# Query and key projections of a pair of heads: seven block products in place of eight

## What is computed

```
hp = rms_norm(xp, norm_mix[0]);  hs = rms_norm(xs, norm_mix[0])
qkv = (xn @ w_qkv).reshape(b, t, 3, N_HEADS, HEAD_DIM)
s = einsum('bqhd,bkhd->bhqk', q, k) * HEAD_DIM ** -0.5 + bias
p = softmax(where(valid, s, neg));  out = einsum('bhqk,bkhd->bqhd', p, v)
x = x + out @ w_o
```

## Time and profile before

| | us |
|---|---|
| median of 3 runs | 1238.0 (1237.76 to 1239.86) |
| profiled execution, its own time | 1235.93 |
| its span in the profile | 1234.1 |
| TensorE busy, over the span | 1059.1 (86%) |
| VectorE busy | 497.5 (40%) |
| ScalarE busy | 295.3 (24%) |
| GpSimd busy | 281.1 (23%) |
| mean granted TensorE clock | 0.944 of 2.4 GHz |

### The profile page before, as it was taken

The page is one execution under the profiler, slowest core; times in us unless marked ns, Lnnn a source line. Parts: engine busy times, 40 slices in busy tenths (PEclk is TensorE's granted clock), DMA queues, the critical chain, the costliest instruction groups (busy, mean ns, idle before and its releaser), DMA issues.

```text
span 1234.1 us, 14547 instructions
## 1 busy us (share of the span) xinstructions
PE 1059.1 (86%) x5320; PEld 619.8 (50%) x5320; DVE 497.5 (40%) x1063; ACT 295.3 (24%) x647; POOL 281.1 (23%) x286
## 2 busy tenths in 40 slices
PE   6999999999997898878874998998996889888880
PEld 5777777776454433333323776764545333333330
DVE  3144434335346311111117598996457111011117
ACT  3223223233211111111002555555111111111002
POOL 3100000000000420110143298990002211110143
PEclk9999999999997998999996998999997999998995
DMA  8973222411716799999995284100018999999994
GB/s 274 383 229 113 78 75 77 131 58 58 314 67 243 276 419 420 420 417 420 420 383 159 75 322 139 50 1 25 35 39 314 406 419 421 390 421 421 420 386 159
DMA packets 109501, 304.79 MB, mean 247 GB/s; under 512 B 17314, under 2 KB 64546, under 8 KB 85737
## 3 DMA queue, kind: packets, MB, share of 16 engines
q1 hardware_dynamic: 87769, 253.95, 53.5%
q0 software_dynamic: 21520, 49.88, 11.1%
q10 hardware_dynamic: 160, 0.26, 0.1%
HBM read 274.94 MB, written 57.38 MB: 269 GB/s over the span
## 4 chain that ended last, share of the span: by engine, by line
PE 58%; DMA 21%; DVE 8%; issue 4%; POOL 4%; ACT 3%; another core or an unknown queue 1%; SPq 0%; POOLq 0%; DVEq 0%; ACTq 0%
DMA arena<-in_w_up 12%; PE bank L1281 11%; PE bank L572 11%; PE bank L471 7%; PE bank L1300 5%; PE bank L1608 5%; DMA ring<-in_w_up 5%; PE bank L599 4%; POOL ring L1782 3%; PE bank L622 2%; PE bank L638 2%; PE bank L663 2%; PE bank L379 2%; DMA work<-in_w_pw 2%; PE bank L1270 1%
## 5 line engine op out<-in xcount | busy, mean ns | idle before, releaser
L1281 PE MATMUL bank<-ring,work 128*64 128x512 f32 x704 | 165.2, 624 | 27.6 <-DMA ring<-in_w_up 25.1
L1300 PE MATMUL bank<-ring,work 128*64 128x512 f32 x512 | 122.0, 620 | 31.4 <-DVE work L1319 21.0
L1608 PE MATMUL bank<-arena,work 128*128 128x256 f32 (+1 forms) x512 | 127.9, 413 | 6.0 <-DMA work<-in_w_pw 4.8
L572 PE MATMUL bank<-arena,ring 128*128 128x288 f32 x512 | 131.9, 412 | 0.0
L1281 PEld LDWEIGHTS bank<-ring,work 128*64 128x64 f32 x704 | 58.0, 143 | 132.1 <-issue 130.8
L1315 DVE TENSOR_TENSOR work<-work,bank 128x256 f32<-128x256 f32 x32 | 13.5, 421 | 271.2 <-ACT work L1311 252.2
L1782 POOL TENSOR_TENSOR ring<-ring 128x576 f32<-128x576 f32 x76 | 107.1, 1409 | 45.0 <-ACT ring L1727 35.7
L1608 PEld LDWEIGHTS bank<-arena,work 128*128 128x128 f32 x512 | 98.7, 193 | 34.6 <-issue 7.4
L572 PEld LDWEIGHTS bank<-arena,ring 128*128 128x128 f32 x512 | 94.9, 190 | 32.6 <-issue 7.9
L471 PE MATMUL bank<-ring,arena 128*128 128x512 f32 x224 | 99.1, 595 | 2.6 <-ACT arena L1766 2.6
L1828 DVE SCALAR_TENSOR_TENSOR bank<-work,ring,bank 128x576 f32<-128x576 f32 x129 | 94.8, 816 | 0.0
(11 more groups left out here) (283 smaller groups left out, 1366.8 us busy)
## 6 DMA issues: line engine op xcount, KB each, us to landing
ring<-in_w_down SPq DMA_DIRECT2D x32, 2048.0 KB, 22.8
ring<-in_w_gate SPq DMA_DIRECT2D x20, 2048.0 KB, 19.8
ring<-in_w_up SPq DMA_DIRECT2D x20, 2048.0 KB, 25.0
arena<-in_w_gate SPq DMA_DIRECT2D x10, 2048.0 KB
arena<-in_w_up SPq DMA_DIRECT2D x8, 2048.0 KB
ring<-in_w_qkv SPq DMA_DIRECT2D x24, 512.0 KB, 6.0
y_sorted<-gain POOLq DMA_DIRECT2D x8, 1536.0 KB, 5.7
work<-in_w_pw SPq DMA_DIRECT2D x16, 512.0 KB, 5.3
```

What stands on the lines that cost most here:

```text
L572: mm = nc.tensor.matmul(bank[b][:, 0:HT], wa[s][:, w, c, :], xt[:, c, h * HT:(h + 1) * HT], start=c == 0, stop=c == C - 1)
L1281: mm = nc.tensor.matmul(bank[2 + s][rr, :], rows_t[:, c, rr], wgu[g][:, :, e, c, :], start=c == 0, stop=c == C - 1)
L1300: mm = nc.tensor.matmul(bank[5 + h][rr, :], hts[:, c, rr], wdn[s][:, e, c, h * HALF:(h + 1) * HALF], start=c == 0, stop=c == FC - 1)
L1608: mm = nc.tensor.matmul(bank[banks[h][w]][:, 0:end - at], wp[s][:, w, c, :], xt[:, c, at:end], start=c == 0, stop=c == C - 1)
```

## The change

The four pieces are a product of two by two blocks: the weights are split into query and key columns and into an upper and a lower half of the 1024 rows (`w_half`), the tokens into two halves (`x_half`). The change computes this with seven products of half the depth (p1 to p7, four matrix products each) in place of eight, in Winograd's form. It needs sums of weights, sums of tokens and sums of products.

- `weight_sums` on GpSimd: per pair four sums of 128 x 512, one of them in place. They wait for the pair's weights (`wa_in`) and for the products of the pair before (`k_mm`). The second and the fourth raise `mixed`, on which p6 and p7 wait.
- `half_sums` on VectorE: once, four sums of 128 x 1152 into `tsum`.
- `joined_products` on VectorE: per pair seven sums of 128 x 288, each of one PSUM bank and one buffer. They take the place of the two key copies. `first_copy` on ScalarE takes p1 out and stands in for the two query copies.
- The scale of 1/8 moves from the query copy into `add_bias`, whose additions become multiply-and-add operations.
- The buffers lie where `wo_sb` lies, so its load moves behind the last join (`k_ev`), on SP's queue too. `slot_rows_dve` moves behind `half_sums`. The last load of `w_pw2` uses the same semaphore.

```diff
+        w_half = [[[wa[s][:, w, m * HC:(m + 1) * HC, :] for m in range(2)] for w in range(2)] for s in range(2)]
+        KMM, KEV = 6, 7
...
+                def product(b, w, t):
+                    for c in range(HC):
+                        mm = nc.tensor.matmul(bank[b][:, 0:HT], w[:, c, :], t[:, c, :], start=c == 0,
+                                              stop=c == HC - 1)
                     return mm
+                (q_lo, q_hi), (diff, k_hi) = w_half[s]
+                if piece == "p1":
+                    pe.wait_ge(wa_in[s], 64 * (k + 1))
+                    pe.wait_ge(v_ev, n)
+                    product(0, q_lo, x_half[0][0]).then_inc(q_mm, 1)
+                if piece == "p6":
+                    pe.wait_ge(v4_ev, n)
+                    pe.wait_ge(mixed, 2 * n + 1)
+                    product(1, wsum[1], tsum[1]).then_inc(k_mm, 1)
+                if piece == "p2":
+                    pe.wait_ge(q_ev, n + 1)
+                    product(0, q_hi, x_half[1][0]).then_inc(k_mm, 1)
+                if piece == "p7":
+                    pe.wait_ge(mixed, 2 * n + 2)
+                    pe.wait_ge(k_ev, KEV * n + 1)
+                    product(1, diff, tsum[2]).then_inc(k_mm, 1)
+                if piece == "p5":
+                    pe.wait_ge(k_ev, KEV * n + 2)
+                    product(0, wsum[0], tsum[0]).then_inc(k_mm, 1)
+                if piece == "p4":
+                    pe.wait_ge(k_ev, KEV * n + 3)
+                    product(1, k_hi, tsum[3]).then_inc(k_mm, 1)
+                if piece == "p3":
+                    pe.wait_ge(k_ev, KEV * n + 5)
+                    product(0, wsum[2], x_half[1][1]).then_inc(k_mm, 1)
...
-                fill("q0")
+                fill("p1", "p6")
-                fill("q1")
+                fill("p2", "p7")
-                fill("k0")
+                fill("p5", "p4")
-                fill("k1")
+                fill("p3")
...
+            def joined_products(n, s, part):
+                q_at, k_at = ([a[s][:, h * HT:(h + 1) * HT] for h in range(2)] for a in (qt, kt))
+                made, b, out, onto, held_by = (
+                    (1, 1, both_prods, first_prod, 0), (2, 0, q_at[0], first_prod, 0), (3, 1, three_prods, both_prods, 1),
+                    (4, 0, k_at[1], three_prods, 3), (4, 0, four_prods, both_prods, 1), (5, 1, k_at[0], three_prods, 3),
+                    (6, 0, q_at[1], four_prods, 5))[part]
+                dve.wait_ge(k_mm, KMM * n + made)
...
+                V.tensor_tensor(out, onto, bank[b][:, 0:HT], ALU.add).then_inc(k_ev, 1)
...
-                    V.tensor_tensor(prob[0:q, b, :, far:nk], psum[0:q, 3:5, far:nk], here(WIN - near, near),
-                                    ALU.add).then_inc(score_free, 1)
+                    V.scalar_tensor_tensor(prob[0:q, b, :, far:nk], psum[0:q, 3:5, far:nk], SCALE,
+                                           here(WIN - near, near), ALU.mult, ALU.add).then_inc(score_free, 1)
...
                 add_bias(n, 0)
+                if more:
+                    joined_products(n + 1, s2, 0)
                 add_bias(n, 1)
                 for t in range(STEPS):
+                    if t == 2 and more:
+                        joined_products(n + 1, s2, KEV - 1)
                     normalise(n, t)
+                    for part in joins.get(t, ()):
+                        joined_products(n + 1, s2, part)
...
+            JOINS_AT = {0: (1, 2), 1: (3, 4, 5)}
+            half_sums()
+            slot_rows_dve(dve, steps)
...
+            sp.wait_ge(k_ev, KEV * PAIRS)
+            sp.dma_start(wo_sb, w_o[0].rearrange("(c p) n -> p c n", p=P)).then_inc(wout_in, 16)
...
+            def weight_sums(n, s, k):
+                (q_lo, q_hi), (k_lo, k_hi) = w_half[s]
+                pool.wait_ge(wa_in[s], 64 * (k + 1))
+                if n is not None:
+                    pool.wait_ge(k_mm, KMM * n)
+                steps.done(pool.tensor_tensor(wsum[0], k_lo, k_hi, ALU.add))
+                steps.done(pool.tensor_tensor(wsum[1], wsum[0], q_lo, ALU.subtract))
+                pool.sem_inc(mixed, 1)
+                steps.done(pool.tensor_tensor(k_lo, q_lo, k_lo, ALU.subtract))
+                pool.tensor_tensor(wsum[2], q_hi, wsum[1], ALU.subtract).then_inc(mixed, 1)
...
+            def pair(n, s, k, more):
+                if more:
+                    weight_sums(n + 2, s, k + 1)
+                store(n, s)
```

More of the change, by code:

```diff
@@ L334, in encoder @@
         raw_in = sem("raw_in"); raw_mm = sem("raw_mm"); raw_ev = sem("raw_ev")
-        wp_in = [sem(f"wp_in{s}") for s in range(2)]; w2_in = sem("w2_in")
+        wp_in = [sem(f"wp_in{s}") for s in range(2)]
         glu_mm = sem("glu_mm"); sig_done = sem("sig_done"); joined = sem("joined"); glu_done = sem("glu_done");
@@ L747, in attn_pe @@
             pe.wait_ge(consts, CONSTS)
-            for piece in ("q0", "q1", "k0", "k1", "kc"):
+            for piece, sums in (("p1", 0), ("p6", 2), ("p2", 0), ("p7", 3), ("p5", 0), ("p4", 4), ("p3", 0), ("kc", 0)):
+                if sums:
+                    pe.wait_ge(halves, sums)
                 project(0, 0, 0, piece)
@@ L758, in attn_act, with first_copy @@
         def attn_act(act, steps):
-            def query_copy(n, s, h):
-                act.wait_ge(q_mm, 2 * n + h + 1)
-                nc.scalar.activation(qt[s][:, h * HT:(h + 1) * HT], bank[h][:, 0:HT], ACT.Copy, scale=SCALE).then_inc(q_ev, 1)
+            def first_copy(n):
+                act.wait_ge(q_mm, n + 1)
+                nc.scalar.copy(first_prod, bank[0][:, 0:HT]).then_inc(q_ev, 1)
             def small_copy(n, s):
@@ L794, in pair @@
                 if more:
-                    query_copy(n + 1, s2, 0)
+                    first_copy(n + 1)
                 exps(n, 1)
-                if more:
-                    query_copy(n + 1, s2, 1)
                 for t in range(STEPS):
@@ L894, in pair @@
                         add_bias(n, t + 2)
-                    if more and t in (1, 2):
-                        key_copy(n + 1, s2, t - 1)
                 if more:
@@ L906, in attn_dve @@
             value4_copy(0, 0, 0, 4)
-            for h in range(2):
-                key_copy(0, 0, h)
+            for part in range(KEV):
+                joined_products(0, 0, part)
             dve.wait_ge(bias_masked, 1)
@@ L981, in attn_pool @@
                                zeros(SLOTS // P + 1 - PAIRS * few)[:, :, 0:HALF]).then_inc(base.y_out[s], 16)
-            with pool.Fori(0, PAIRS // 2) as it:
+            def pair(n, s, k, more):
+                if more:
+                    weight_sums(n + 2, s, k + 1)
+                store(n, s)
+                pool.dma_start(y_rows[:, dyn(n * few, few), :], zeros(few)).then_inc(zeros_in, 16)
+            weight_sums(1, 1, 0)
+            PER = 2 * 3
+            with pool.Fori(0, PAIRS // 2 - 1) as it:
+                steps.enter(it, PER)
                 for s in range(2):
-                    store(2 * it + s, s)
-                    pool.dma_start(y_rows[:, dyn((2 * it + s) * few, few), :], zeros(few)).then_inc(zeros_in, 16)
+                    pair(2 * it + s, s, it, True)
+            steps.leave(PAIRS // 2 - 1, PER)
+            for s in range(2):
+                pair(PAIRS - 2 + s, s, PAIRS // 2 - 1, False)
         def logits_at(j):
```

78 lines of the change are left out of this document (38 added, 40 removed).

## The result

| | before | changed |
|---|---|---|
| median of the runs, us | 1237.88 (1237.38 to 1239.86, 4 runs) | 1250.27 (1249.36 to 1253.18, 4 runs) |
| profiled execution, its own time | 1235.93 | 1249.36 |
| span | 1234.1 | 1247.7 |
| mean granted TensorE clock | 0.944 | 0.936 |

The ratio is 1.0104, with an interval of 1.0085 to 1.0122: the change makes the kernel about 1% slower. The forecast of 1236.0 has the wrong sign, and the time lies above the range of 1227 to 1247.

A forecast was written before the change was run, and what follows sets the result against it. Attention was taken as paced by TensorE alone. Start +1.5, six pairs at -0.43 (-2.6), the seventh -1.21 and last pair +0.24 gave -2.1 us: 1233.8 profiled, 1236.0 as median; range 1227 to 1247.

The forecast's parts named there:

- Products, joins, copies: Projections: four products fewer each, 1.94 us; joins covered except the last; third transposition 1.21 earlier per pair if nothing holds the scaling.
- without exclusion: Rival one, third step's scaling: GpSimd's sums do not delay it; seven pairs gain 1.21 each, 1228.2 us; chance 35%.
- Do GpSimd and VectorE exclude each other?: Scaling ahead of the third transposition: waits for one whole GpSimd sum, so a pair gains 0.43 us instead of 1.21.
- the forecast's own case: Pairs with weight sums: one GpSimd sum holds the scaling, gain 0.43 us a pair; chance 37%.
- The point between forecast and rival two: Scalings, one per head: whether a waiting GpSimd sum goes ahead of VectorE's queued second scaling; forecast took that it does not.
- rival two: Scalings: GpSimd gets in twice, third transposition 0.89 us later in six pairs; +7.3, 1245.4 us; chance 22%.
- the 1.5 and 2.8 that I had named: TensorE's wait on the scaling at a pair's third transposition: 1.5 us in the forecast, 2.8 in rival two.
- Pair 0: Ahead of the loop: GpSimd's and VectorE's sums take turns; first scores at 46.7 to 50.3 instead of 46.29, taken as +1.5 us.
- GpSimd's price: Weight sums: 1.27 us each, 0.16 between them, four take 5.6 us; time alone hides them.
- Last pair and output weights: Last pair: multiply-and-adds add 0.12 us at two transpositions, +0.24; output weights' load has 15.8 us, needs 10.0.
- rival three: Output weights' load, now behind the last join, comes late: 1 to 3 us on any case; 6% together with the rest.
- Carried through unchanged: After attention everything hangs on attention's end, so a shift of that end passes through to the total unchanged.

The follow-up runs named there:

- run 1: Changed kernel with GpSimd's stores of a pair and its zero store ahead of the weight sums; 1232.84 us, 0.996 of the kernel before.
- run 7: Changed kernel with the first weight sum of a pair in place and the other three behind the stores; 1234.44 us, ratio 0.9973.
- run 6: Kernel before, plus only four GpSimd sums of 128x512 per pair into a spare tile, started at the fourth step's scores; 1239.01 us, ratio 1.0006.
- run 3: Changed kernel plus four useless products between the fill p3 and the third transposition, sums left beside the scalings; 1242.5 us, ratio 1.0033.
- run 2: run 1 with the loop's weight sums left out, waits and signals kept, stale sums used; 1222.45 us, ratio 0.9866, total not comparable.
- run 4: run 1 with the last join behind the scaling of step 2 instead of ahead of it; 1229.51 us, ratio 0.9923.
- run 8: run 4 plus three extra VectorE additions into a spare tile ahead of each third reciprocal; 1252.67 us, against 1239.56 for the kernel before.
- run 9: run 4 plus four extra VectorE additions into a spare tile ahead of each third reciprocal; 1259.05 us.

## Why the prediction was wrong

Two steps failed. The forecast let one GpSimd sum hold the scalings where two do, so a pair loses 0.46 instead of gaining 0.43, about 5 us over six pairs; and it had no term for TensorE's clock, which cost 8 us.

- **Products, joins, copies.** Right in the main. 448 records; every join but the last is covered; 1.09 per pair without exclusion (run 1), predicted 1.21; the seventh pair gained 1.17. Gain and wait of a pair add up to 1.71 (1.09 + 0.62 in run 1, 0.63 + 1.08 in run 7, 2.17 - 0.46 in the changed kernel), where the forecast had 1.94: some 0.2 us a pair are lost besides the wait. The traces show 0.06 of it, the transpositions after a wait (0.66 for 0.60); where the rest goes no run shows.
- **"Do GpSimd and VectorE exclude each other?"** Yes, and with a size that was right: run 7, the forecast's own case, gains 0.63 a pair, predicted 0.43. The difference is mostly the end of a held scaling, which comes some 0.15 behind the sum and not 0.3 and more.
- **The point between forecast and rival two.** This step failed. I gave 22% to "a waiting GpSimd sum goes ahead of the second scaling", against it that "the second scaling needs no semaphore". It goes ahead every time: second scaling 1414 ns in the changed kernel, 1422 in run 6. Rival two's mechanism is what happened, with its size too large: the transposition is later by 0.46 a pair and not 0.89, since the second sum starts 0.09 behind the first (rival two let it wait for the end of the first scaling, 0.32 behind) and the held scaling ends 0.15 behind its sum (0.40 in rival two). The wait was 2.17, between the 1.5 and 2.8 that I had named.
- **The clock.** No case had this term, and it is the largest: five pairs by 1.6, 8 us of the 12.4. I read the granted clock as 1.00 in the earlier trace rows and carried it into cases in which TensorE would stand idle for up to 2.8 us. Without it the changed kernel would have come at about 1242, as run 3 did. That is inside the range, though still slower than before; the clock alone took the time out of the range.
- **Pair 0.** Forecast +1.5 from p6 at 34.1, p7 from 38.1 and scores from 46.7; measured p6 at 33.89, p7 at 38.99, scores at 47.65, +1.36. The mechanism is right, the engines take turns, but the number is luck. The trace of the changed kernel had its last copy at 25.52 where the earlier trace rows has 26.76. From that copy to the first scores it takes 22.13 instead of 19.53, so the change costs 2.6 us here (22.0 to 22.3 in runs 1 to 4, 8 and 9; 21.3 in run 7). I had gone near the lower end, since the small operations are 0.17 each; three of them are held for 1.12 and more:

```profile
30.26 2.31 DVE L848 TENSOR_TENSOR ring<-arena,ring 128x1152 f32<-128x1152 f32 x1
32.60 1.12 DVE L1174 TENSOR_SCALAR row_bits<-tok_at 128x16 int32<-128x16 int32 x1
```

```profile
29.42 1.94 POOL L1009 TENSOR_TENSOR ring<-ring 128x512 f32<-128x512 f32 x1 [13.35 <-DMA work<-in_cache_attn_k]
31.43 2.26 POOL L1010 TENSOR_TENSOR ring<-ring 128x512 f32<-128x512 f32 x1
```

- **GpSimd's price.** Forecast 1.27 with 0.16 between sums; measured 1.26, with 0.09, 0.18 and 0.08 between the four. Right.
- **Last pair and output weights.** +0.24 was forecast, 0.0 measured (26.76 both times). The waits there are the same as before: 0.18 at the third transposition, as in the earlier trace rows, and 1.00 at the fourth. The first output product starts at 303.53, 0.53 behind the scores, without a wait, so rival three did not occur.
- **After attention.** "Carried through unchanged" holds to 915 to 919 us, a scatter of the size of some of the effects, which is why the pairs' lengths decide here and not the totals.

## What to carry to other kernels

Before a product is taken out of a fill, subtract it from the slack of the chain that runs beside it, and put nothing in the chain's last microseconds that can hold it: here the same sums cost 17 us in one place of GpSimd's order and nothing in another. Count every GpSimd operation over SBUF that is queued there, not only the first, since each can go ahead of one more VectorE operation. And where TensorE would newly stand idle for 2 us or more within an otherwise full stretch, add a term for its clock (here 1.6 us each time it fell), or fill the gap: four useless products made the kernel 8 us faster. Several waits of about 1 us close together need the same care.

## What the runs showed of the hardware

- GpSimd additions with both inputs in SBUF (128x512, 1.26 us) hold VectorE's one-input SBUF scalings for whole sums, and VectorE's two-input additions hold them in turn: at the start 1.36 becomes 2.31 and 1.26 becomes 2.26. A queued GpSimd sum goes between two scalings of VectorE that stand back to back. The Trainium skill, "SBUF — State Buffer", section "Who interferes with whom", says that whoever issues first gets the shared pair for the whole instruction and that the other blocks fully; the 823 and 1414 ns of the two scalings agree. That two engines which both have work take turns one by one, so that a short operation pays a long one each time, the runs show beyond it.
- Operations of VectorE with one tensor in PSUM are not held: the joins beside a sum take 0.45 as before.
- Small integer operations of VectorE of 128x16 were held for 1.12, 1.20 and 1.13 us in the changed kernel, two others between them, which started in a pause of GpSimd, took 0.18 and 0.17.
- TensorE's clock fell to its lower level with a wait of 2.14 to 2.17 us in ten of thirteen pairs (changed kernel and run 8), with 2.87 us in six of seven, and with one wait of 1.08 to 1.19 us or of 0.62 us in none (runs 7 and 1), nor with the one of 1.61 in run 6. It fell in three of the eleven traces with waits of 1.00, 1.10 and 0.84 us in a row at the end of attention. The fall came between 0.5 us before the end of the wait (run 9) and 1.6 us behind it (changed kernel), and lasted some 3 us, in one pair of run 9 twice that (the pair of 39.24).
